# Neighbourhood attention with query and key tiles in pairs, and each pair's heads inside the next pairs' tiles

## The reference, cut to what matters

```python
z = rmsnorm(h, na_norm[j]) @ na_w_qkv[j]
h = h + neighbourhood_attention(z, na_q_g[j], na_k_g[j], na_rpb[j]) @ na_w_out[j]

# neighbourhood_attention
q = split(rmsnorm(z[..., :D].reshape(B, L, H, dh), q_g) * (dh ** -0.5))
k = split(rmsnorm(z[..., D:2 * D].reshape(B, L, H, dh), k_g))
v = split(z[..., 2 * D:])
s = jnp.einsum('bhqd,bhrqwd->bhqrw', q_i, k_win).astype(jnp.float32)
s = s + jnp.transpose(bias, (0, 2, 1, 3)).astype(jnp.float32)[None]
pr = jax.nn.softmax(s.reshape(B, H, GRID_W, kh * kw), axis=-1).reshape(B, H, GRID_W, kh, kw)
return jnp.einsum('bhqrw,bhrqwd->bhqd', pr.astype(v.dtype), v_win)
```

## Time and profile before

| | |
|---|---|
| time, median of 3 runs | 2971.44 us (2969.02 to 2972.38) |
| profiled execution | 2971.91 us, of which the traced span is 2970.6 us |
| granted clock, mean | 0.994 |
| PE busy | 2869.7 us (97% of the span) |
| DVE busy | 1699.9 us (57%) |
| ACT busy | 603.4 us (20%) |
| chain that ended last | PE 91%, DVE 5%, ACT 3%, issue 1% |

### The profile page before, as it was taken

How to read it: one execution, slowest core, us unless ns; L and a number is a source line. 1 busy time by engine, 2 the same in 40 slices (tenths; PEclk the granted TensorE clock), 3 DMA queues, 4 the chain that set the end, 5 groups by cost and what they waited for, 6 DMA issues and landing times.

```text
span 2970.6 us, 41131 instructions
## 1 busy us (share of the span) xinstructions
PE 2869.7 (97%) x16774; PEld 2361.2 (79%) x16774; DVE 1699.9 (57%) x3407; ACT 603.4 (20%) x1372; POOL 37.4 (1%) x60
## 2 busy tenths in 40 slices
PE   8988999998999999999999999999999999999999
PEld 7777788984889978888644468888888888765999
DVE  3376467335467477773225457775377773235775
ACT  1254221134221120000123520100020000134110
POOL 0000000020000000000000000000000000000000
PEclk9999999999999999999999999999999999999999
DMA  6400474662565644422223034442444433322444
GB/s 237 138 2 3 146 236 146 192 185 85 181 224 141 195 156 160 157 87 78 79 61 114 1 115 159 164 125 59 118 169 157 147 87 78 114 82 86 143 145 112
DMA packets 344015, 376.15 MB, mean 127 GB/s; under 512 B 7219, under 2 KB 292292, under 8 KB 343060
## 3 DMA queue, kind: packets, MB, share of 16 engines
q1 hardware_dynamic: 318548, 285.68, 31.3%
q10 hardware_dynamic: 23072, 82.52, 7.7%
q0 software_dynamic: 2208, 5.31, 0.9%
HBM read 372.44 MB, written 1.05 MB: 126 GB/s over the span
## 4 chain that ended last, share of the span: by engine, by line
PE 91%; DVE 5%; ACT 3%; issue 1%; DVEq 0%; POOL 0%; ACTq 0%; POOLq 0%
PE acc L134 75%; PE aux L134 14%; ACT sb_xn L302 1%; PE aux L2429 1%; DVE sb_work L1569 1%; DVE sb_work L2073 0%; DVE sb_work L2070 0%; DVE sb_big L1399 0%; DVE sb_xn L278 0%; DVE sb_work L1399 0%; DVE sb_work L2084 0%; ACT sb_rstd L290 0%; ACT sb_rstd L292 0%; ACT sb_work L2537 0%; ACT sb_big L1086 0%
## 5 line engine op out<-in xcount | busy, mean ns | idle before, releaser
L134 PE MATMUL acc<-sb_xn,weights 128*128 128x256 f32 (+3 forms) x5184 | 1215.1, 388 | 20.1 <-DVE sb_xn L278 10.8
L134 PEld LDWEIGHTS acc<-sb_xn,weights 128*128 128x128 f32 (+1 forms) x5184 | 943.1, 190 | 244.9 <-issue 121.0
L134 PE MATMUL acc<-sb_work 128*128 128x256 f32 (+1 forms) x1944 | 374.1, 346 | 2.9 <-DVE sb_work L1574 2.9
L134 PEld LDWEIGHTS acc<-sb_work 128*128 128x128 f32 x1944 | 323.6, 191 | 38.1 <-issue 4.0
L134 PE MATMUL acc<-sb_work,weights 128*128 128x256 f32 (+2 forms) x1508 | 322.2, 361 | 6.2 <-DVE sb_work L1616 3.9
L134 PE MATMUL acc<-sb_big,weights 128*128 128x256 f32 (+1 forms) x1776 | 316.5, 335 | 4.0 <-issue 3.9
L134 PEld LDWEIGHTS acc<-sb_big,weights 128*128 128x128 f32 x1776 | 280.6, 193 | 30.8 <-issue 5.3
L134 PEld LDWEIGHTS acc<-sb_work,weights 128*128 128x128 f32 x1508 | 254.1, 191 | 54.6 <-issue 26.7
L1536 ACT COPY sb_work<-acc 128x256 f32<-128x256 f32 (+1 forms) x108 | 36.7, 339 | 683.9 <-PE acc L134 683.9
L1609 DVE TENSOR_TENSOR sb_work<-sb_work,acc 128x256 f32<-128x256 f32 (+1 forms) x112 | 42.5, 379 | 217.9 <-PE acc L134 217.9
L134 PE MATMUL aux<-sb_xn,sb_work 128*128 128x256 f32 (+1 forms) x704 | 148.6, 354 | 0.1
(11 more groups left out here) (347 smaller groups left out, 2683.0 us busy)
## 6 DMA issues: line engine op xcount, KB each, us to landing
weights<-ffn_w_up SPq DMA_DIRECT2D x88, 1024.0 KB, 9.0
weights<-ffn_w_down SPq DMA_DIRECT2D x48, 1408.0 KB, 7.2
sb_work<-w_mod_rows ACTq DMA_DIRECT2D x100, 512.0 KB, 6.1
weights<-ffn_w_gate SPq DMA_DIRECT2D x44, 1024.0 KB, 5.5
sb_big<-w_mod_rows ACTq DMA_DIRECT2D x44, 512.0 KB, 4.8
weights<-mix_w_in SPq DMA_DIRECT2D x6, 2048.0 KB, 12.2
weights<-na_w_qkv SPq DMA_DIRECT2D x6, 2048.0 KB, 9.9
weights<-ple_w_gate SPq DMA_DIRECT2D x4, 2048.0 KB, 8.1
```

The costliest lines, as they stand in the source:

```text
L134: return te.matmul(o, lhsT, rhs, start=start, stop=stop, skip_group_check=True)
```

## The change

The order of the stage is new, the operations on the data are the same. The weight blocks of queries and keys are cut differently: each of four blocks holds two query tiles and the two key tiles of the same heads, by two transfers, and the first value block is loaded second. Dense groups take two `acc` banks, 0 and 1; banks 2 and 3 hold scores, one for each head of a pair, so a head's scores wait for the bias addition two heads earlier. PE makes query tile 0, key tile 0, two value tiles, then the pairs 1 to 7, then the other two value tiles. In pair p's tiles, after four of the eight steps, it places what is ready of earlier pairs: the sum of squares of the tile before, the transposes of head 2p-3 and the scores of pair p-1; between the two tiles the transposes of head 2p-4, behind them the values of pair p-2. The scores of a pair are now issued head by head, each with its own waits. All sums of squares use `aux[2]`; a sum waits until the one before has been read. Transposes alternate between two banks instead of three. The turned heads get more room (`na_pt`, 14 places instead of 4), of which heads 8 to 13 lie in `big`. The values of pairs 5 and 7 go to `aux[2]`, the others to `aux[3]`. POOL issues the bias transfers head by head, the mask first, under four semaphores; DVE waits for four heads at a time. ACT's reload of its function table before the exponentials is gone. The lists of ACT and DVE follow PE's order.

```diff
-    def next_group(numbered=None):
-        bank = n_groups[0] % 4
+    def next_group(numbered=None, banks=4):
+        bank = n_groups[0] % banks
...
-            self.qk = wide_plan(2 * D)
-            groups = flat(self.qk)
...
-            self.v = [block(2) for _ in range(2)]
+            pairs = [open_block(2)]
+            values = [open_block()]
+            for i in range(8):
+                if i and i % 2 == 0:
+                    pairs.append(open_block(2))
+                for _ in range(2):
+                    next_group(pairs[-1], 2)
+                if i == 0:
+                    for _ in range(2):
+                        next_group(values[0], 2)
...
+        pair(0)
+        value(0)
+        for i in range(1, 4):
+            pair(i)
+        value(1)
         sync_wide(N.proj, ins["na_w_out"][0])
...
+        def tile(p, kind, between=()):
...
+            for k in range(KT):
...
+                if k == 4:
+                    for step, at in between:
+                        step(at)
+                ins_ = mm(acc[g.bank][:, 0:L], t(k, c, c + 128), xv_l[:, k, :], k == 0, k == KT - 1)
+            acc_full.on(ins_)
...
+        def square_sum(j):
+            te.wait_ge(hn_sq.sem, N.heads.at[0](j))
+            if j:
+                te.wait_ge(hn_rstd.sem, N.heads.at[2](j - 1))
+            hn_sum.on(mm(aux[2][:, 0:L], blk64[:], na_sq[:, j % 2, :]))
+
+        def scores(n):
+            p, hp = divmod(n, 2)
+            r = slice(64 * hp, 64 * hp + 64)
             te.wait_ge(na_qh_set.sem, N.qh(p))
...
+            te.wait_ge(hn_scaled.sem, N.heads.at[3](2 * p + 1))
+            if n < 2:
+                te.wait_ge(acc_free[2 + n].sem, N.score_banks[n])
+            else:
+                te.wait_ge(at_bias.sem, N.biased(n - 2))
             for t in range(2):
...
+                ins_ = mm(acc[2 + hp][:, L * t:L * t + L], na_qh[r, p, 128 * t:128 * t + 128], na_qk[r, 8 + p, :])
+            at_sc.on(ins_)
...
+        tile(0, 0)
+        tile(0, 1, [(square_sum, 0)])
+        value_tile(0, 0)
+        value_tile(0, 1)
+        for p in range(1, KT):
+            tile(p, 0, [(square_sum, 2 * p - 1)])
+            if p > 1:
+                turn(2 * p - 4)
+            tile(p, 1, [(square_sum, 2 * p)] + ([(turn, 2 * p - 3)] if p > 1 else []) + [(scores, 2 * p - 2), (scores, 2 * p - 1)])
+            if 2 <= p < 6:
+                values(p - 2)
+        value_tile(1, 0, [(square_sum, 15), (turn, 12)])
+        turn(13)
+        scores(14)
+        scores(15)
+        value_tile(1, 1)
+        turn(14)
+        values(4)
+        turn(15)
+        for p in range(5, KT):
+            values(p)
         tensor_wide(N.proj, lambda k: na_o[:, k, :], lambda k: (at_out, N.out(k)))
...
+        for p in range(1, KT):
+            rstd(2 * p - 1)
+            tile(p, 0)
+            if p > 1:
+                turned(2 * p - 4)
+            rstd(2 * p)
+            if p > 1:
+                turned(2 * p - 3)
+            tile(p, 1)
+            exponentials(2 * p - 2)
+            reverse(p)
+            exponentials(2 * p - 1)
+            if 2 <= p < 6:
+                heads_out(p - 2)
...
+        for p in range(1, KT):
+            if p > 1:
+                divide(2 * p - 4)
+            scale(2 * p - 1)
+            if p > 1:
+                divide(2 * p - 3)
+            square(2 * p)
+            mask(2 * p - 2)
+            mask(2 * p - 1)
+            scale(2 * p)
+            biased_max(2 * p - 2)
+            square(2 * p + 1)
+            biased_max(2 * p - 1)
```

More of the change, by code:

```diff
@@ L1949, in tensor_neighbours, with value_tile @@
+            acc_full.on(ins_)
+        def value_tile(b, tt, between=()):
+            blk, g = N.v[b], N.v[b].groups[tt]
             te.wait_ge(weights_in[blk.slot].sem, blk.arrived_at)
+            te.wait_ge(acc_free[g.bank].sem, g.free_at)
             t = k_tiles(blk.slot, 0, KT, 512)
[L1951 to L1954, removed]
@@ L1956, in scores @@
-        def scores(p):
-            te.wait_ge(na_qh_set.sem, N.qh(p))
[L1959 to L1965, removed]
-            for t in range(2):
[L1967 to L1971, removed]
+            for k in range(KT):
+                if k == 4:
+                    for step, at in between:
+                        step(at)
+                ins_ = mm(acc[g.bank][:], xv_l[:, k, 128 * tt:128 * tt + 128], t(k, 0, 512), k == 0, k == KT - 1)
@@ L1987, in tensor_neighbours @@
[L1987 to L2001, removed]
@@ L2018, in scalar_neighbours @@
[L2018 to L2034, removed]
-                    p = m // 2 - 1
-                    ac.wait_ge(at_val.sem, N.val(p))
-                    src = aux[3][:, L * (p % 2):L * (p % 2) + L].rearrange("p (r c) -> p r c", c=GRID_W)[:, :, ::-1]
-                    at_out.on(ac.copy(na_o[:, p, :].rearrange("p (r c) -> p r c", c=GRID_W), src))
@@ new lines, in reverse, with exponentials @@
+        def reverse(p):
+            ac.wait_ge(hn_scaled.sem, N.heads.at[3](2 * p))
+            na_qh_set.on(ac.copy(na_qh[:, p, :].rearrange("p (r c) -> p r c", c=GRID_W)[:, :, ::-1],
+                                 na_qk[:, p, :].rearrange("p (r c) -> p r c", c=GRID_W)))
+        def exponentials(n):
+            ac.wait_ge(at_neg.sem, N.neg(n))
+            for i in range(2):
+                e = na_e[:, n % 4, L * i:L * i + L]
+                ins_ = ac.activation(e, e, ACT.Exp, bias=na_st[:, n % 4, 2 + i:3 + i], scale=1.0,
+                                     accum_out=na_st[:, n % 4, 4 + i:5 + i])
+                (at_exp if i else a_step).on(ins_)
@@ L2044, in vector_neighbours @@
+        turned(12)
+        turned(13)
+        exponentials(14)
+        exponentials(15)
+        turned(14)
+        heads_out(4)
+        turned(15)
+        for p in range(5, KT):
+            heads_out(p)
     def vector_neighbours(N):
@@ new lines, in vector_neighbours @@
+        value_tile(0, 1)
+        for p in range(1, KT):
[11 more added lines that the diff above has]
+            biased_max(2 * p - 1)
+        divide(12)
+        scale(15)
+        divide(13)
+        mask(14)
+        mask(15)
```

200 lines of the change are left out of this document (122 added, 78 removed).

## The result

| | before | after |
|---|---|---|
| median of 11 and of 6 runs on one chip | 2969.65 us | 2954.36 us |
| ratio, 95% interval | | 0.9952 (0.9937 to 0.9966) |
| profiled execution, span | 2971.91, 2970.6 us | 2955.26, 2953.8 us |
| first query tile to first projection matmul | 132.74 us | 116.65 us |
| from there to the end of the span | 2225.2 us | 2227.2 us |

The first series gave 2954.41 us against 2969.02, ratio 0.9950 (0.9935 to 0.9965). So the change gains 15 us, by the interval 10 to 19. I forecast 2958.3, 13.1 less than before, with a range that ended at 2954.5.

A forecast was written before the change was run, and what follows sets the result against it. The stage was taken as bound half by PE, half by DVE. PE's 115.1 us + 2.4 + 1.4 + 0.5 + 0.2 = 119.6 against 132.7, 13.1 less: 2958.3 us, range 2955 to 2961, lower end 2954.5, upper 2966.

The forecast's parts named there:

- What bounds the kernel; the order: In the stage, dense tiles are bound by PE and heads by DVE; heads laid beside tiles leave PE's 115.1 us plus extras.
- PE's bare work, 115.1: Stage's tiles, square sums, value tiles, transposes, values and scores, priced from PE's timeline, sum to 115.1 us in any order.
- Scores, +2.4: Issuing a pair's scores head by head costs 1.3 us instead of 1.0, for eight pairs 2.4 us more.
- The row of the recurrence: Recurrence's first products: second row half begins some 0.5 us late with 16 instructions ahead, 0.03 us for each.
- Rival 1: A pair's two heads' scores run one behind the other, 1.83 us instead of 1.3: +4.2 us, 2962.5; chance 0.17.
- Rounds, +1.4: PE waits 0.2 us in each of the stage's seven pair rounds, 1.4 us in all.
- the last part, +0.5: At the stage's end, values wait for DVE's copy of the last value tile: 0.4 us, entered as 0.5.
- The walk along the loop: From key tile's end to next query's square, the chain takes 6.7 us against PE's 7.2 of cover: half a microsecond left.
- Rival 3's threshold: Slower: waiting mid query tile every round decides from 2.1 us a round; at 2.5 the time is 2974.4; chance 0.05.
- Bias, masks, loads, square sums in one bank: In the stage, bias and mask transfers, weight loads and the single sum bank cost nothing; next FFN's loads near 709 and 725.
- rival 4: No change: the next FFN waits for its weights and the 13 us are given back, 2971; chance 0.04.
- No low clock any more: In the stage, PE no longer has the long wait that preceded the 1.2 GHz stretch, so no clock fall is expected.

The follow-up runs named there:

- the heads-behind kernels: Changed kernel with all heads behind the dense tiles: transposes ahead of scores 3017.61 us, stage 179.77; scores first 2971.99 us, stage 137.96.
- Five copies: Changed kernel with five extra ACT copies ahead of the Ln of each of pairs 2 to 7: 2972.50 us, stage 130.18.
- the steps at the tiles' ends: Changed kernel with earlier pairs' steps moved from mid-tile to behind each whole tile: 2949.26 us, again 2956.43 (6 runs); stage 119.00 and 119.02.

## Why the prediction was right, and where it was not

*What bounds the kernel; the order.* Right. One half bound by PE and one by DVE became one stretch in which PE works 116.25 of 116.65 us; DVE and ACT do the same work beside it. That the cover is the cause is read from PE's waits, 12.0 us for the division before and none after; the heads-behind kernels agree, since they keep the new banks and the issue by head and have no gain, but they lose a pair's overlap or the clock besides.

*PE's bare work, 115.1.* 116.65 with everything. Tiles were 1.9 us more than forecast: 0.3 of waits, and the change of shape at each piece of small work, four times 0.19 where scores stand on one side of a half tile and values on the other, three times 0.10 behind scores alone and four times 0.10 behind values. I had priced a tile as one piece. Transposes were 1.05 less, and 1.45 less without the 0.4 us of wait among them: my 0.59 was read between values and scores (717.89 to 718.48) and holds the change of shape; ahead of a dense tile they cost 0.44, ahead of scores 0.53.

*Scores, +2.4.* This term failed by size: the pair takes 1.07 us, not 1.3, close to the lower bound of 1.0, and the eight pairs 8.57 us where I had 10.4. The row of the recurrence pointed the right way, and I scaled its distance of 0.03 us per instruction ahead to a case where it is 0.013 for all four. Rival 1 is out. Forced by a wait, the same order cost 2.31 a pair where I had put 1.83, 0.3 of it the wait's hand-over. The rule of the Trainium skill's page "TensorE: Matmul & The Clock Gate" (Part 3, "The mechanism"), that matmuls start strictly in program order, doesn't agree with the two starts within 0.03 us shown above.

*Rounds, +1.4, and the last part, +0.5.* 0.28, mis-sized too, and 0.4. The walk along the loop was sound: a slack of 0.78 us in the four middle rounds where I said 0.5. Charging 0.2 a round over a positive slack was caution and no reading. What the walk missed is that the first and the last round have none.

*Rival 3's threshold.* From 2.1 us of wait a round on the change should lose. Five copies, 2.15 us longer, gave 2972.5 against 2971.5 for the kernel before beside it, one execution each, which can't tell a microsecond. By the stage, 130.18 against 132.74, the change was still 2.6 us ahead; its loss was 9.9 us of waits and 3.6 of clock, which my threshold didn't have.

*Bias, masks, loads, square sums in one bank.* No wait of PE for any of them; the next FFN's loads leave from 705.13 us on, where I had said 709, and rival 4 didn't come. *No low clock any more* held in the profile that came with the result; in two others the stage's first tile ran at 0.50.

*The step that failed, and what put the time outside the range.* The forecast, 2958.3, lies 3.9 us above the first series' median. Of these, 3.0 are the stage, 116.65 us for 119.6: the scores' term was 1.8 us too large and the rounds' 1.1, while the smaller errors of the other rows nearly cancel. The other 0.9 is the base, which came out 2.4 us lower, while 1.5 us of the stage's gain don't show in the medians: I subtracted from the median of three runs, 2971.4, and gave it no width, though the runs of the kernel before go from 2963.2 to 2976.3 us and their median came down to 2969.02 and 2969.65 with more runs. It took both: with the measured stage on the forecast's base the time would be 2955.3, with the forecast's stage on the measured base 2955.9, and either is inside the range. That they fell the same way is chance. How far executions differ, the code ahead of the stage shows; two stretches of it, in before and then with the steps at the tiles' ends:

```profile
100.00:200.00 100.00, 91.66 (x912) 71.20 (x914) 59.30 (x113) 41.31 (x81) 0.00 (x0) 0.95 0.19 64
500.00:560.00 60.00, 58.96 (x513) 58.96 (x513) 33.09 (x50) 2.93 (x10) 0.00 (x0) 0.96 0.54 152
```

```profile
100.00:200.00 100.00, 90.11 (x1074) 70.64 (x1072) 63.48 (x125) 42.77 (x86) 0.00 (x0) 1.00 0.20 65
500.00:560.00 60.00, 60.00 (x538) 59.85 (x536) 29.61 (x54) 3.08 (x10) 0.00 (x0) 1.00 0.55 154
```

Same code, clock 0.95 and 0.96 against 1.00, and the first tile comes 9.3 us later in the first; some 6 of these arise in the two stretches.

## What to carry to other kernels

Where one stretch is bound by the dense engine and its neighbour by a loop over the others, put the loop inside the dense tiles: the gain is what the dense engine's bare work leaves of the stage, less the changes of shape, here 16.1 of 17.6 us, and both can be read ahead. Walk the loop against its cover for the first and the last round too, and price small work in the middle of a tile by the change of shape it brings. Give the base of a sum the scatter of the runs as its width, and judge a mechanism by its stage.

## What the runs showed of the hardware

- Matmuls on the two row halves overlap fully when one half's four stand ahead of the other's in the program: 1.07 us a pair, as alternating, against 2.31 in series with a wait between them; the second half starts 0.013 us behind the first.
- A change between full-size matmuls and those of half height (scores) or half width (values) costs about 0.1 us a time (0.31 us from start to start instead of 0.216).
- Behind a wait of 1.6 us the clock was granted at 0.50 for 5.4 us in one execution and at 1.00 in another of the same kernel: 2.7 us. Where such falls come varies from execution to execution; idle matmuls were followed by 1.00 in all three waits tried, but without them so were 11 of 13 waits ahead of the stage and 8 of 12 ahead of the FFN behind it, so three don't show that they hold the clock, and the whole time didn't fall.
